# One of four expert rows is scaled by ScalarE and added by GpSimd instead of being summed by TensorE, in 127 of 272 turns

## The reference, cut to what matters

```
x   = x + (ga * branch_a + gb * branch_b) @ w_out
xn  = rmsnorm(x) * norm_ffn
q   = xn @ w_q                                  # 8 heads
sc, eidx = top 16 of the sums of two key scores # per head, 16384 experts
g   = softmax(sc)
act = gelu(sum(u_tab[eidx] * xn))               # one number for each chosen expert
x   = x + sum over 8 heads and 16 picks of (g * act) * v_tab[eidx]
y   = rmsnorm(x) * norm_final
```

## Time and profile before

| what | value |
|---|---|
| median of 3 runs | 3387.22 us (3382.61 to 3388.38) |
| the profiled execution | 3387.77 us, span 3385.6 us |
| instructions in the profile | 33356 |
| mean granted TensorE clock | 0.984 |
| DMA moved | 1311.20 MB, mean 387 GB/s |
| gathers | 1088, 1140.92 MB |
| slabs and the rest of SyncE's queue | 167.36 MB |

### The profile page before, as it was taken

One profiled execution on the slowest core, in us unless ns is written; L12 is line 12 of the kernel. 1 busy time (PEld: TensorE's weight loads), 2 busy tenths in 40 slices (PEclk: granted clock), 3 DMA queues, 4 the chain that ended last, 5 costly groups with the idle time before them and its releaser, 6 DMA issues.

```text
span 3385.6 us, 33356 instructions
## 1 busy us (share of the span) xinstructions
PE 3120.1 (92%) x10016; PEld 1786.2 (53%) x10016; DVE 2420.4 (71%) x5476; ACT 1218.0 (36%) x4064; POOL 1430.1 (42%) x1244
## 2 busy tenths in 40 slices
PE   8999999999999999999999999999999777777776
PEld 6877565555555565655555565655554232322232
DVE  8826998666678798666678798665688666666664
ACT  4223443243333443333333443333333333233332
POOL 1202355444444365343444455343334554445453
PEclk9999999999999999999999999999999999999999
DMA  4357999999999999999999999999999999999998
GB/s 137 106 180 290 376 409 418 419 418 419 416 415 416 398 408 417 418 416 417 406 413 418 402 413 418 419 418 419 414 410 384 420 420 420 403 420 420 419 410 332
DMA packets 209604, 1311.20 MB, mean 387 GB/s; under 512 B 23632, under 2 KB 28880, under 8 KB 70160
## 3 DMA queue, kind: packets, MB, share of 16 engines
q0 software_dynamic: 156672, 1140.92, 82.2%
q1 hardware_dynamic: 51472, 167.36, 13.1%
q10 hardware_dynamic: 1280, 0.79, 0.1%
HBM read 1298.34 MB, written 10.64 MB: 387 GB/s over the span
## 4 chain that ended last, share of the span: by engine, by line
PE 59%; DMA 22%; DVE 11%; issue 3%; ACT 3%; POOL 1%; POOLq 0%; DVEq 0%; SPq 0%; ACTq 0%
PE ps_acc L784 32%; DMA rows<-in_experts,idx 22%; PE ps_a L596 15%; DVE rows L1468 5%; PE ps_a L686 4%; PE ps_v L596 4%; PE ps_a L713 1%; DVE va L1302 1%; ACT coef L953 1%; PE ps_y L653 1%; PE ps_a L690 1%; ACT diag L957 1%; POOL rows L1647 1%; PE ps_v L635 1%; PE ps_v L697 0%
## 5 line engine op out<-in xcount | busy, mean ns | idle before, releaser
L784 PE MATMUL ps_acc<-rows,diag 128*128 128x512 f32 x4352 | 2000.1, 608 | 229.9 <-ACT diag L957 228.4
L1647 POOL DMA_INDIRECT rows<-in_experts,idx x1088 | 1302.7, 1197 | 1688.0 <-PE ps_acc L784 1417.6
L1468 DVE CUSTOM_DVE_ANT_0 rows<-rows,xn 128x1024 f32<-128x1024 f32 x1088 | 1323.8, 1230 | 752.1 <-DMA rows<-in_experts,idx 740.5
L784 PEld LDWEIGHTS ps_acc<-rows,diag 128*128 128x128 f32 x4352 | 820.0, 193 | 1261.3 <-issue 868.0
L950 ACT ACTIVATE act_v<-dots 128x2 f32<-128x2 f32 x544 | 110.5, 203 | 1752.7 <-DVE dots L1468 1746.3
L957 ACT ACTIVATE diag<-pk,coef 128x128 f32<-128x128 f32 x1088 | 377.2, 394 | 17.7
L596 PE MATMUL ps_a<-xnT,ring 128*128 128x272 f32 x1536 | 372.7, 397 | 0.9 <-issue 0.8
L596 PEld LDWEIGHTS ps_a<-xnT,ring 128*128 128x128 f32 x1536 | 295.0, 193 | 92.0 <-issue 34.0
L953 ACT ACTIVATE coef<-act_v,soft 128x1 f32<-128x1 f32 x1088 | 261.4, 287 | 17.8
L1302 DVE SCALAR_TENSOR_TENSOR va<-va,pk 128x302 f32<-128x302 f32 x480 | 259.6, 603 | 0.5
L596 PE MATMUL ps_a<-gates,ring 128*128 128x272 f32 x1024 | 246.3, 394 | 2.3 <-ACT sig L924 1.4
(11 more groups left out here) (268 smaller groups left out, 1996.4 us busy)
## 6 DMA issues: line engine op xcount, KB each, us to landing
ring<-in_slabs SPq DMA_DIRECT2D x256, 512.0 KB
rows<-in_experts,idx POOLq DMA_INDIRECT x1088
ring<-made_slabs SPq DMA_DIRECT2D x24, 512.0 KB
xt<-in_x_prompt SPq DMA_DIRECT2D x4, 1024.0 KB, 13.9
out_y_prompt<-yt SPq DMA_DIRECT2D x8, 512.0 KB
ring<-made_slabs SPq DMA_DIRECT2D x12, 256.0 KB
made_slabs<-rows SPq DMA_DIRECT2D x1, 2048.0 KB, 9.5
made_slabs<-rows SPq DMA_DIRECT2D x4, 512.0 KB, 9.2
```

Of the source, the lines that this page charges most:

```text
L784: ins = pe.matmul(ps_acc[:, h, :], diag[:, slot, :], rows[:, slot, D + h * 512:D + (h + 1) * 512], start=first, stop=False, skip_group_che ...
L1468: ins = dve.tensor_tensor_reduce(rows[:, slot, 0:D], rows[:, slot, 0:D], xn[:, :], 1.0, 0.0, ALU.mult, ALU.add, dots[:, s:s + 1])
L1647: pool.indirect_dma_start(out=rows[:, slot, :], out_offset=None, in_=experts, in_offset=bass.IndirectOffsetOnAxis(ap=idx[:, a, k:k + 1], a ...
```

## The change

A constant `ADDED_TURNS` names 127 turns: in group 0 turns 3 to 9 and 20 to 55, in groups 1 and 2 turns 4 to 9 and 20 to 55, none in the last group or the sample turns. In each, slot 1 of the four is an added slot. For it ScalarE scales the v half in place by the coefficient, where it made a diagonal before, and raises `scaled_done`. GpSimd adds the scaled half to the residual rows `x2t` of the tile (`add`), behind the first two gathers of the turn, and raises `slot_added`. TensorE sums the other three slots. The gather that reuses the place of an added slot waits for `slot_added`, the others for `slot_free`, whose counts no longer have an initial 9 and leave out the added slots (`summed`). VectorE's sum at the end of the tile waits for both.

```diff
+ADDED_AT = 1
+ADDED_TURNS = ((*range(3, 10), *range(20, 56)), (*range(4, 10), *range(20, 56)), (*range(4, 10), *range(20, 56)), ())
+
+def added(i):
+
+    turn, k = divmod(i, STEPS)
+    g, t = divmod(turn, TURNS)
+    return g < GROUPS and k == ADDED_AT and t in ADDED_TURNS[g]
+
+ADDED = [0]
+for slot_number in range(ALL_TURNS * STEPS):
+    ADDED.append(ADDED[-1] + added(slot_number))
+
+def summed(i):
+
+    return i - ADDED[i]
...
                 for s in range(s0, s1):
                     slot, first = place(n, s)[0], s == 0 and n % TPAIRS == 0
+                    if added(PAIR * n + s):
+                        continue
                     if first and n:
                         pe.wait_ge(y_sum, n // TPAIRS)
-                    pe.wait_ge(diag_done, PAIR * n + s + 1)
+                    pe.wait_ge(diag_done, summed(PAIR * n + s + 1))
...
             pe.wait_ge(kept_in, 16)
-            pe.sem_inc(slot_free, RING)
             pe.sem_inc(y_done, 2)
...
                 for s in range(b * BATCH, (b + 1) * BATCH):
+                    if added(PAIR * n + s):
+                        scaled = rows[:, place(n, s)[0], D:2 * D]
+                        act.activation(scaled, scaled, ACT.Copy, scale=coef[:, s:s + 1]).then_inc(scaled_done, 1)
+                        continue
                     act.activation(diag[:, place(n, s)[0], :], shape, ACT.Copy, scale=coef[:, s:s + 1]).then_inc(diag_done, 1)
...
                 dve.wait_ge(y_out, 16 * t + 16)
-                dve.wait_ge(slot_free, RING + steps)
+                dve.wait_ge(slot_free, summed(steps))
+                if ADDED[steps]:
+                    dve.wait_ge(slot_added, ADDED[steps])
...
-                    pool.wait_ge(slot_free, PAIR * n + s + 1)
+                    used = PAIR * n + s - RING
+                    if used >= 0 and added(used):
+                        pool.wait_ge(slot_added, ADDED[used + 1])
+                    elif used >= 0:
+                        pool.wait_ge(slot_free, summed(used + 1))
...
+            def add(n, r):
+
+                i = PAIR * n + STEPS * r + ADDED_AT
+                if not added(i):
+                    return
+                t, slot = n // TPAIRS, place(n, i - PAIR * n)[0]
+                if ADDED[i]:
+                    pool.wait_ge(slot_added, ADDED[i])
+                pool.wait_ge(xn_ready, t + 2)
+                pool.wait_ge(scaled_done, ADDED[i + 1])
+                pool.tensor_tensor(x2t[:, t % 2, :], x2t[:, t % 2, :], rows[:, slot, D:2 * D], ALU.add).then_inc(slot_added, 1)
...
                     if n < LAST_PAIR or r < PTURNS - 2:
                         ahead(n, r, b)
+                    if b == 0:
+                        add(n, r)
```

More of the change, by code:

```diff
@@ L369, in program @@
         slot_free = sem("slot_free")
+        slot_added = sem("slot_added")
+        scaled_done = sem("scaled_done")
         gathers = sem("gathers")
```

## The result

The changed kernel takes 3400.8 us (median of 6 runs, 3398.6 to 3401.8) against 3388.1 for the kernel before beside it (6 runs, 3382.6 to 3390.1). The ratio is 1.0035, interval [1.0025, 1.0045]: slower by 12.7 us. The forecast was 3368.0; the time lies outside the range, 5.8 us above its upper end, and 2.8 us from rival 2's 3398.

The account below looks back on a forecast made before the run. It took the DMA engines' 419 GB/s as floor, with 37.5 us lost above it by window, mostly to PE. Gains of 7.0 + 3.6 + 2.5 + 4.5 + 1.2 + 1.0 = 19.8 us gave 3387.8 - 19.8 = 3368.0; range 3350 to 3395.

Parts of the forecast that it names:

- rival 2: DVE becomes the bound in group 0's turns 3 to 9 and entering turns 10 to 19: +10 us, 3398; chance 0.15.
- turns behind 11 (442, 1192, 1943): Windows starting at these microseconds, limited by DVE; 1.2 of 5.4 us lost was to come back.
- middles (492, 1291, 1991): Long mid-group windows starting at these microseconds; 1.0 of 2.6 us lost was to come back.
- The point from which rival 2 decides: An add costing DVE over 1.7 us on average, since lateness carried into turns 10 to 19 can't be caught up.
- group 0's early turns at nothing: Turns 4 to 11 of group 0: PE's relief against DVE's price, between +8.0 and -4.5 us, taken as 0.
- half of the price: Group 0, turns 4 to 11: DVE at 96.3 of 99 us, PE at 86; at best likely a gain of 2.7.
- price by window: DVE's busy time plus up to 2.4 us per add, against each window's DMA floor; all fit but group 0's turns 4 to 11.
- these losses are PE's: Windows 1571 to 1710 (3.6 us lost) and 2366 to 2549 (3.5): PE always busy, DVE a third free.
- 4.5 us at the last group's start: Turns 0 to 3, 2549 to 2596 us: 4.5 of 6.6 us lost to PE's backlog was to come back.
- some 10 us less late: How much earlier PE was to enter the last group's first four turns, at 2549 us.
- slot 4r+10: Its gather, set free by the add and queued behind it, was to leave some 2 us later against PE's slot 4r.
- rival 1: The ring doesn't fill: add and its wait for a dot hold back gathers of 4r+10 and 4r+11; 3380 to 3392, chance 0.17.

Follow-up runs that it names:

- relief_only: Changed kernel without GpSimd's add, ScalarE still scaling, 127 rows left out of the output; 3380.04 us against 3387.04 for the kernel before, 0.9976.
- add_only: Kernel before plus GpSimd's add in the same 127 turns, written over the dead half of the slot, TensorE summing every slot; 3411.97 us, 1.0072.
- no_early: Changed kernel without the adds in turns 3 to 9 of group 0, 120 adds; 3391.23 us, 1.0010 against the kernel before.
- middle: Changed kernel with adds only in turns 20 to 51 of the first three groups, 96 adds; 3388.07 us against 3388.26 for the kernel before, 0.9997.
- relief_all: As relief_only, but slot 1 left out in every turn from 3 or 4 to 63, 181 rows; 3379.35 us against 3386.70 for the kernel before, 0.9978.
- fill_only: As add_only, but three GpSimd fills of the dead half, reading nothing, in place of each add; 3389.12 us, 1.0008 against the kernel before.
- light_dots: Kernel before with VectorE's dots over 512 columns in the groups' last four and first four turns; 3386.79 us against 3386.70, 0.9999.
- the halves: Changed kernel with each add split into two of 512 columns so a dot can come between; 3403.43 us, 1.0050 against the kernel before.

## Why the prediction was wrong

The table has the loss of each window against 419.5 GB/s, cut at the landings themselves to a tenth of a microsecond, and what the sum had forecast to get back of it. Positive is a gain on the kernel before. Behind each column stands one profiled execution, and an entry is good to some 0.3 us.

```
                                     forecast  after  relief_only  add_only
turns 4-11, groups 1 and 2              7.0     3.5       3.2         2.0
turns 44-55, group 1 (1571)             3.6     3.5       3.5         3.6
turns 48-63, group 2 (2366)             2.5    -0.8       0.8         1.3
turns 0-3, last group (2549)            4.5    -0.1       0.2         0.6
turns behind 11 (442, 1192, 1943)       1.2    -4.1       0.7       -12.8
middles (492, 1291, 1991)               1.0    -4.1      -1.6       -13.5
turns 4-11, group 0 (343)               0.0    -2.7       3.8        -5.5
group 1 turn 56 to group 2 turn 3       0.0    -5.7      -4.0        -0.1
sum                                    19.8   -10.5       6.6       -24.4
```

**What was right.** The work: 3844 matmuls of slot sums; adds of 2.41 us where 2.4 was taken; 7.2 us of GpSimd work a turn. ScalarE's scale takes 1133 ns and not 1050, off the path. That an add can take its whole length from VectorE was read from one overlap, and the runs bear it out, 1.87 of 2.41 us on average. The Trainium skill, "SBUF — State Buffer", the section on the two separate sides, calls this an exclusive lock for the whole instruction, against a GpSimd operation that reads; the dots of 3.93 and 3.76 us are such holds, and fills leave the dots at 1231 ns. It gives the lock to whichever operation starts first; by the starts recorded here that isn't always so, since the dot at 381.22 began 0.48 us ahead of the add and was the one held. The point from which rival 2 decides, 1.7 us an add, was passed by 0.17, and its time is right within 2.8 us. That nearness is in part luck: it had 5.5 us in group 0's early turns and 5 us at each of the three entries, less gains of 10, while no_early puts 8.5 to 9.6 us on group 0's early turns and leaves 3 to 4 for all the rest.

**The step that failed first: group 0's early turns at nothing.** The working had 103.5 us of VectorE's work for a window of 99 and a bound of +4.5. It then tried half of the price, for which it shows no row, and took zero. The window took 102.3 us, and the four turns behind it, where VectorE had 49.0 of 50 busy before, some 5 us more. The price of lateness belongs to this step: the sum counted a window's own DVE time, and a window behind it that has no room pays for it too. no_early gives 8.5 to 9.6 us for these seven adds. The share that an add costs VectorE, 1.87 of 2.41 over the whole kernel, is 78% and not half. The prediction counted the top lists as one-input work that an add leaves alone; the operation of L1472 shows that a part of them is held as well.

**The same step in the middles.** The prediction gave them +1.0, after its price by window had found that VectorE's work and the adds fit into the DMA floor by their sums. They lost 4.1 us in the change and 13.5 in add_only; middle, whose adds stand in turns 20 to 51 alone, lost 4.5 there as well, and got it back in other windows. So a sum that fits doesn't make a hold free. That a dot 2.7 us late frees its place late wherever it stands is the likely way, argued and not shown by a run.

**The second: adding up what PE can give back.** Each window's loss was taken as a gain for itself. Relief alone gives 6.6 us of 19.8, and 3.8 of these in the one window that was put at zero. 3.5 us at turns 44 to 55 do come back, and 4.0 are lost again from turn 56 of group 1 to turn 3 of group 2, where no slot is taken from PE. The other 54 slots, which relief_all takes in turns 10 to 19 and 56 to 63, don't make the kernel faster. So "these losses are PE's" was too much to read from a PE that is never idle. add_only says the same from the other side: at turns 44 to 55 of group 1 it loses 0.2 us instead of 3.8 though PE has all its work. One reading is that its turns before are slower and PE comes there with less behind it; but fill_only and light_dots, with all of PE's work too and as fast as before, lose 1.6 and 1.7 us there. So part of such a loss moves from window to window, and the loss of a window in one execution isn't an amount that can be got back.

**The third: 4.5 us at the last group's start.** The mechanism, PE's backlog coming due, is a part of it at most. Waits of the gather queue from 35 us before that start to 13 us behind it, the stretch of the earlier trace rows, after the change and in relief_only:

```profile
POOL rows L1681 <- PE ps_acc L809: 25.0, 10, 5.4
```

```profile
POOL rows L1679 <- PE ps_acc L809: 22.2, 7, 5.4
```

25.0 us where 25.3 stood: turns 56 to 63 have no adds, and the places wait for PE as long as before. With the relief up to turn 63, relief_all gets 2.5 us, and the same stretch still has 23.0 us of such waits with the turns ahead at 419 GB/s; so the row that the prediction read as PE's backlog isn't a measure of it. For PE's entering "some 10 us less late" the prediction gives no working. Relieved of 508 matmuls, PE waited longer for diagonals instead, 378 us in the whole kernel against 228.

**Covers.** The prediction had the gather of slot 4r+10 leave some 2 us later against PE's slot 4r. A turn of no_early in the timeline:

```profile
1116.68 1.99 POOL L1681 DMA_INDIRECT rows<-in_experts,idx  x1 [2.76 <-PE ps_acc L809]
1118.70 2.38 POOL L1696 TENSOR_TENSOR x2t<-x2t,rows 128x1024 f32<-128x1024 f32 x1
1121.88 1.12 POOL L1681 DMA_INDIRECT rows<-in_experts,idx  x1 [0.81 <-PE ps_acc L809]
```

The gather behind the add is out at 1123.00, 6.3 us after the first one began and 7.1 after PE had done with slot 4r, against 3.6 in the kernel before: 3.5 us and not 2. The pause of 0.81 us, which stands behind 124 of the 127 adds of the change, was not in the price. fill_only holds the queue as long, with the same pause behind the last fill, and loses 2 us in the whole kernel, so rival 1 had little to stand on.

**What the parts leave open.** The add costs 25 us alone and the relief gives 7; together that would be 18 slower, and 12.7 are measured (11.9 by the ratio). Rows five and six of the table show where they are not additive: behind turn 11 and in the middles add_only loses 26 us and the change 8. That a late dot hurts less where PE is early would explain it; it is an argument from the windows, and no run separates it.

## What to carry to other kernels

Before work is moved off an engine, run the kernel with that work simply left out: here it would have said 7 us where the sum of window losses said 20. When the work's new place makes another engine wait while it runs, as GpSimd's two-input add does to VectorE's two-input work, charge most of the work's length (78% here) to that engine, also where its busy time would fit, and look at the stretch behind as well as the one it stands in. A loss while an engine is never idle need not be that engine's own: here the relief brought some of it back and it came up again in later turns. And look in the trace whether an edit did what it was for before its time is read: the halves left almost no gap for a dot.

## What the runs showed of the hardware

GpSimd's add of two 128x1024 tiles costs VectorE 1.87 us on average and a dot that meets it up to 2.8 (4.05 at the most, instead of 1.23). The add takes 2.36 us in the median; 22 of the 127 take 2.5 us or more, up to 2.96, each of them with a dot recorded as begun 0.47 to 0.95 us ahead of it and not held. So either waits for the other. Fills of as many columns on GpSimd (957 ns each) cost VectorE's dots nothing: 1231 ns with 381 of them.

PE's granted clock fell when PE was relieved: its mean was 0.984 in the 3385.6 us of before and is 0.968 in the 3396.7 us of after. With two levels, 2.4 GHz and half of it, this is 2 x (1 - 0.984) x 3385.6 = 108 us at 1.2 GHz before and 217 us after; add_only, which takes nothing from PE, has 0.984, and relief_only 0.973. In the rows of after it is lowest in windows in which PE has gaps (0.92 at 1715, 0.94 at 343 and 1858, 0.95 at 1105 and 1298) and 0.99 or 1.00 where it has hardly any. The share of gaps alone doesn't set it: the last group of before has 0.96 with PE busy 184 of 240 us. The slot sums' matmuls, 608 ns before, take 624. PE's busy time fell by 150 us and not by the 229 of the sum. The matmuls of a slot sum start 429 ns apart at the full clock and 853 at half (medians, in both traces), so 109 us more at half are up to 54 of the difference. Turns 4 to 11 of group 0, where the change lost first, hold 12 us of half clock after and 3 before. Whether the clock has a part in that loss, or in the relief's small worth, no run tells apart.
